# Two decoder layers with routed experts on one core: later row ids, a split first gate/up product, 112-column slot tables

## The reference

```python
scores = jax.nn.sigmoid(xt @ router_w)               # 512 tokens x 16 experts
group  = argmax over 4 groups of the sum of the two best biased scores
expert_idx = the two best experts of that group      # 2 of 16 for each token
w = scores[expert_idx]; w = w / sum(w)
for e in range(16):
    h = silu(xt @ w_gate[e]) * (xt @ w_up[e])        # 1024 -> 512
    y = y + gates[:, e:e + 1] * (h @ w_down[e])      # 512 -> 1024
```

## Time and profile before

| | |
|---|---|
| Median of 3 runs | 1144.84 us (1144.48 to 1145.73) |
| The profiled execution: its own time | 1144.45 us |
| Its span, first to last instruction | 1142.8 us |
| TensorE (PE) busy | 1105.0 us, 97% |
| VectorE (DVE) busy | 836.7 us, 73% |
| ScalarE (ACT) busy | 663.3 us, 58% |
| GpSimd (POOL) busy | 89.7 us, 8% |
| Granted TensorE clock, mean | 0.993 |
| DMA | 295.96 MB, 259 GB/s over the span |

### The profile page before, as it was taken

The page is one execution under the profiler, slowest core; times in us unless marked ns, Lnnn a source line. Parts: engine busy times, 40 slices in busy tenths (PEclk is TensorE's granted clock), DMA queues, the critical chain, the costliest instruction groups (busy, mean ns, idle before and its releaser), DMA issues.

```text
span 1142.8 us, 15358 instructions
## 1 busy us (share of the span) xinstructions
PE 1105.0 (97%) x5434; PEld 872.0 (76%) x5434; DVE 836.7 (73%) x1023; ACT 663.3 (58%) x761; POOL 89.7 (8%) x104
## 2 busy tenths in 40 slices
PE   6999999899999999999999999999989999999995
PEld 5888888567777777777888888888757777777773
DVE  4543556789999999988616555536779999998996
ACT  4322323568888888863417332213548888887872
POOL 2000000111111111010000000000101111111113
PEclk9999999999999999999999999999999999999998
DMA  9925421699999999987304222430499999999985
GB/s 337 384 74 221 147 93 52 217 360 404 382 382 388 378 387 382 391 280 253 134 32 169 89 74 83 169 118 37 154 327 372 388 374 386 381 370 389 378 274 148
DMA packets 51752, 295.96 MB, mean 259 GB/s; under 512 B 8932, under 2 KB 9092, under 8 KB 22128
## 3 DMA queue, kind: packets, MB, share of 16 engines
q1 hardware_dynamic: 35232, 249.58, 57.1%
q0 software_dynamic: 9328, 21.96, 6.9%
q10 hardware_dynamic: 7136, 23.71, 5.5%
HBM read 277.07 MB, written 29.62 MB: 268 GB/s over the span
## 4 chain that ended last, share of the span: by engine, by line
PE 88%; DMA 6%; DVE 3%; ACT 1%; issue 1%; ACTq 0%; DVEq 0%; SPq 0%; POOLq 0%
PE ps L481 26%; PE ps L483 26%; PE ps L482 26%; DMA X<-y_rows 4%; PE ps L1918 2%; PE ps L2133 1%; PE ps L2001 1%; PE ps L1824 1%; DMA y_rows<-y,odx 1%; PE ps L1941 1%; PE ps L1842 1%; DVE lo L477 1%; DMA raw<-in_w_moe 1%; PE ps L1813 1%; DVE hot L518 1%
## 5 line engine op out<-in xcount | busy, mean ns | idle before, releaser
L477 DVE TENSOR_TENSOR lo<-raw,hi 128x1024 fp32r<-128x1024 f32 x320 | 378.6, 1221 | 90.6 <-ACT hi L466 89.1
L466 ACT ACTIVATE hi<-raw 128x1024 fp32r<-128x1024 f32 x320 | 331.2, 1058 | 135.0 <-PE ps L483 99.0
L481 PE MATMUL ps<-hi,xgT_hi 128*112 128x512 f32 x480 | 190.6, 397 | 0.0
L483 PE MATMUL ps<-hi,xgT_lo 128*112 128x512 f32 x480 | 189.1, 394 | 0.0
L482 PE MATMUL ps<-lo,xgT_hi 128*112 128x512 f32 x480 | 187.9, 391 | 0.0
L477 DVE TENSOR_TENSOR lo<-raw_more,hi 128x1024 fp32r<-128x1024 f32 x128 | 154.9, 1222 | 15.9 <-ACT hi L466 7.9
L466 ACT ACTIVATE hi<-raw_more 128x1024 fp32r<-128x1024 f32 x128 | 134.6, 1058 | 33.9 <-PE ps L483 23.3
L481 PE MATMUL ps<-xT_hi,hi 128*128 128x512 f32 x320 | 127.5, 398 | 8.9 <-DVE lo L477 8.9
L482 PE MATMUL ps<-xT_lo,hi 128*128 128x512 f32 x320 | 125.4, 392 | 0.0
L483 PE MATMUL ps<-xT_hi,lo 128*128 128x512 f32 x320 | 125.3, 392 | 0.0
L483 PEld LDWEIGHTS ps<-hi,xgT_lo 128*112 128x112 f32 x480 | 84.0, 175 | 26.4
(11 more groups left out here) (209 smaller groups left out, 1445.2 us busy)
## 6 DMA issues: line engine op xcount, KB each, us to landing
raw<-in_w_moe SPq DMA_DIRECT2D x128, 1024.0 KB, 10.5
raw_more<-in_w_moe SPq DMA_DIRECT2D x64, 1024.0 KB, 10.8
raw<-in_w_dense SPq DMA_DIRECT2D x39, 1024.0 KB, 5.6
y_rows<-X ACTq DMA_DIRECT2D x4, 2048.0 KB, 24.9
X<-y_rows POOLq DMA_DIRECT2D x12, 512.0 KB, 11.6
x_rows<-X ACTq DMA_DIRECT2D x8, 512.0 KB, 2.6
xT_raw<-in_x_t SPq DMA_DIRECT2D x4, 512.0 KB, 6.4
X<-in_x SPq DMA_DIRECT2D x1, 2048.0 KB, 10.0
```

Source lines behind the costliest of these rows:

```text
L466: nc.scalar.activation(hi[:, s, :], flat(raw_units(n)), ACT.Copy).then_inc(hi_ready, 1)
L477: eng.tensor_tensor(lo[:, s, :], flat(raw_units(n)), hi[:, s, :], ALU.subtract).then_inc(lo_ready, 1)
L481: nc.tensor.matmul(out_, a_hi, b_hi, start=first, stop=False)
L483: return nc.tensor.matmul(out_, a_lo, b_hi, start=False, stop=last)
```

## The change

Five things, in both layers:

1. `other_ids` and `route_ids(layer, False)` go. `gates_to_slots` multiplies all 7 columns of `tok_par` instead of 4, and `slot_gates` reads all 7 and makes `idx` of experts 3 to 15 too. POOL's fetch of expert 3 and all after it wait for that.
2. In `gate_up_first`, units 0 to 5 are multiplied as before; then `turn_x(1)` comes, then the gate halves of units 6 and 7, then their up halves. `silu(0)` waits for the gate halves alone (`half_done`), `hidden(0)` for all.
3. `sum_by_slot` takes 112 columns of a table as weights, and `slots_hot` writes 112 of each 128; what follows works on 112 partitions.
4. ACT issues the two DMAs of `ffn_par` after the loop over the experts, just ahead of the last turns, instead of at the start of the experts.
5. Order on ACT and VectorE: `x_hi(1)`, `silu(0)`, the split of unit 4 of expert 1, `h_hi(0)`, then the splits of units 5 to 7. `route_gates` is cut in two: its first four instructions (`gate_values`) come ahead of `hidden(0)`, the other nine (`gate_parts`) where it was.

```diff
         def slots_hot(eng, out_, pos, t, es=slice(0, E)):
-            return eng.tensor_tensor(out_[:, es, :], iota_s[:, None, :].to_broadcast([P, n, P]),
-                                     pos[:, t, es, None].to_broadcast([P, n, P]), ALU.is_equal)
+            return eng.tensor_tensor(out_[:, es, 0:T], iota_s[:, None, 0:T].to_broadcast([P, n, T]),
+                                     pos[:, t, es, None].to_broadcast([P, n, T]), ALU.is_equal)
...
                 def silu(c, step=0, i=0):
-                    act.wait_ge(unit_used, at(INDEX, gu0(layer, c) + GU - 1, step, i) + 1)
+                    if is_zero(c):
+                        act.wait_ge(half_done, 2 * layer + 1)
+                    else:
+                        act.wait_ge(unit_used, at(INDEX, gu0(layer, c) + GU - 1, step, i) + 1)
...
                 preload(ACT.Silu)
-                params(layer, 1, ffn_par[layer])
...
-                for k in range(4, GU):
-                    split_hi(act, gu0(layer, 1) + k)
                 x_hi(1)
                 silu(0)
+                split_hi(act, gu0(layer, 1) + 4)
                 h_hi(0)
+                for k in range(5, GU):
+                    split_hi(act, gu0(layer, 1) + k)
...
+                params(layer, 1, ffn_par[layer])
                 load = heavy(act, layer)
                 last_turns()
...
             def slot_gates(layer):
                 dve.wait_ge(gates_by_slot, layer + 1)
-                chain.step(nc.vector.tensor_copy(scr[layer]["by_slot"][:, :, 3:7],
-                                                 ps[:, 7, 0:4 * E].rearrange("p (e a) -> p e a", a=4)))
+                chain.step(nc.vector.tensor_copy(scr[layer]["by_slot"][0:T, :, :],
+                                                 ps[0:T, 7, 0:7 * E].rearrange("p (e a) -> p e a", a=7)))
+                rows_by_slot(chain, layer, slice(NA, E)).then_inc(idx_ready, 1)
+                dve.wait_ge(idx_ready, 2 * layer + 2)
                 out_rows(chain, layer)
...
-                route_ids(layer, False)
                 route_most(layer)
                 x_lo(1)
+                gate_values(layer)
                 hidden(0)
-                for k in range(4, GU):
+                own_lo(gu0(layer, 1) + 4)
+                h_lo(0)
+                for k in range(5, GU):
                     own_lo(gu0(layer, 1) + k)
-                h_lo(0)
-                route_gates(layer)
+                gate_parts(layer)
...
-                    ins = nc.tensor.matmul(ps[:, bank, n * e:n * (e + 1)], onehot[:, e, :],
+                    ins = nc.tensor.matmul(ps[0:T, bank, n * e:n * (e + 1)], onehot[:, e, 0:T],
...
             def gates_to_slots(layer):
                 pe.wait_ge(gates_done, layer + 1)
                 for t in range(NT):
-                    ins = sum_by_slot(hot[layer][t], 7, t, 3, 4)
+                    pe.wait_ge(hot_ready, 2 * NT * layer + NT + t + 1)
+                    ins = sum_by_slot(hot[layer][t], 7, t, 0, 7)
...
-                    for k in range(GU):
-                        n = gu0(layer, 0) + k
-                        wait_raw(pe, n)
-                        for h in range(2):
-                            ins = nc.tensor.matmul(...)
-                        ins.then_inc(unit_used, 1)
+                    for k in range(GU - 2):
+                        wait_raw(pe, gu0(layer, 0) + k)
+                        product(k, 0)
+                        product(k, 1).then_inc(unit_used, 1)
                         if k == 4:
                             counts(layer)
-                            other_ids(layer)
-                        if k == GU - 2:
-                            turn_x(1)
+                    turn_x(1)
+                    wait_raw(pe, gu0(layer, 0) + GU - 1)
+                    product(GU - 2, 0)
+                    product(GU - 1, 0).then_inc(half_done, 1)
+                    for k in (GU - 2, GU - 1):
+                        product(k, 1).then_inc(unit_used, 1)
```

More of the change, by code:

```diff
@@ L490, in hybrid_decoder @@
         IDA = (7, 3)
-        IDR = (3, 7)
         NA = 3
@@ L526, in rows_by_slot @@
-            return nc.vector.scalar_tensor_tensor(out=idx[:, es], in0=by[:, es, 0], scalar=no_row[:, 0:1],
-                                                  in1=by[:, es, 1], op0=ALU.add, op1=ALU.add)
+            chain.step(nc.vector.scalar_tensor_tensor(out=by[0:T, es, 0], in0=by[0:T, es, 2], scalar=no_row[0:T, 1:2],
+                                                      in1=by[0:T, es, 0], op0=ALU.mult, op1=ALU.add))
+            return nc.vector.scalar_tensor_tensor(out=idx[0:T, es], in0=by[0:T, es, 0], scalar=no_row[0:T, 0:1],
+                                                  in1=by[0:T, es, 1], op0=ALU.add, op1=ALU.add)
@@ L601, in expert @@
                 q = e + E * (turn - 1)
[L602 to L605, removed]
+                src = idx[0:T, e:e + 1] if isinstance(e, int) else idx[0:T, bass.ds(e, 1)]
+                chain.post(nc.gpsimd.tensor_copy(idx_col[0:T, 0:1], src))
+                dst = odx[0:T, e:e + 1] if isinstance(e, int) else odx[0:T, bass.ds(e, 1)]
+                chain.step(nc.gpsimd.tensor_copy(out_col[0:T, 0:1], dst))
                 used = q * EP
@@ L1423, in place_slots, with route_ids @@
                 slots_hot(dve, hot[layer][t], posm, t, slice(0, NA)).then_inc(hot_ready, 1)
[L1425 to L1429, removed]
-                                                 ps[:, bank, 3 * es.start:3 * es.stop].rearrange("p (e a) -> p e a", a=3)))
+            def route_ids(layer):
+                es, bank = slice(0, NA), IDA[layer]
+                dve.wait_ge(ids_ready, layer + 1)
+                chain.step(nc.vector.tensor_copy(scr[layer]["by_slot"][0:T, es, 0:3],
+                                                 ps[0:T, bank, 3 * es.start:3 * es.stop].rearrange("p (e a) -> p e a", a=3)))
                 rows_by_slot(chain, layer, es).then_inc(idx_ready, 1)
@@ L1437, in route_most, with gate_values @@
                 nc.vector.tensor_copy(most[:, layer:layer + 1], scr[layer]["most_f"][:, :]).then_inc(most_ready, 1)
-            def route_gates(layer):
+            def gate_values(layer):
                 gates, gsum = scr[layer]["gates"], scr[layer]["gsum"]
@@ L1493, in hidden @@
                     dve.wait_ge(silu_ready, plus(c + m0 + 1, i))
+                    if is_zero(c):
+                        dve.wait_ge(unit_used, gu0(layer, 0) + GU)
                     if c + m0:
@@ L1853, in first_ids @@
                     ins.then_inc(ids_ready, 1)
-            def other_ids(layer):
-                for t in range(NT):
-                    pe.wait_ge(hot_ready, 2 * NT * layer + NT + t + 1)
-                    ins = sum_by_slot(hot[layer][t], IDR[layer], t, 0, 3, range(NA, E))
-                ins.then_inc(ids_ready, 1)
             def counts(layer):
```

31 lines of the change are left out of this document (16 added, 15 removed).

## The result

| | before | after |
|---|---|---|
| Median of 3 runs | 1144.84 us | 1164.16 us (1163.16 to 1166.40) |
| The profiled execution: own time, span | 1144.45, 1142.8 us | 1163.16, 1161.5 us |
| PE, DVE, ACT, POOL busy | 1105.0, 836.7, 663.3, 89.7 us | 1109.7, 837.6, 665.0, 111.6 us |

A forecast was written before the change was run, and what follows sets the result against it. The prediction took TensorE, 88% of the chain, as the bound, with the DMA also full. Terms of -2.7 us (layer 0) and -3.5 (layer 1) made -6.2, so 1138.6 us on the median's scale; range 1133.3 to 1143.0.

The forecast's parts named there:

- What waits for those ids later: POOL's fetch of expert 3 waits for slot_gates: margin some 3 us, cost nothing, up to 1 us if slow.
- What it saves there is kept to the end, if nothing else holds it: Start of the experts: TensorE never stops once the pipeline runs, so time saved there lasts to the end.
- my sum: Terms of both layers added: -2.7 us in layer 0, -3.5 in layer 1, together -6.2 us.
- The tail: Layer ends: late ffn_par's 1 MB meets the last scatter; 0.7 us taken in each layer, between 0 and 2.
- this rival: Layer ends: last scatter shares the DMA with ffn_par and lands late, 5.0 us lost per layer: 1147.2 us, chance 0.06.
- Weight loads: gates_to_slots: 64 matmuls with 112-column weights take 3.8 us instead of 1.63, 2.2 us more in each layer.
- The rival that they hide: gates_to_slots: dearer weight loads overlap matmuls, so 4.4 us more are gained: 1134.2 us, chance 0.12.
- The clock: Falls behind layer 0's stop and layer 1's turn_h(0) counted as gone, 1.7 us each; least certain of the gains.
- falls elsewhere: Clock falls behind the longer gates_to_slots stretch in both layers, 1.7 us each: 1142.0 us, chance 0.17.
- the stop of `other_ids`: Start of experts: row ids of experts 3 to 15 leave TensorE's path, gaining 3.3 us in each layer.
- the wait before `turn_h(0)`: TensorE's stop falls to 0.8 us: 0.6 less in layer 0, 1.4 in layer 1; gate_values nothing, at worst 0.3.
- The weights don't follow: Later experts: the full DMA's weight ring sets TensorE's arrival, losing the start's gain: about 0, 1144.8 us, chance 0.10.

The follow-up runs named there:

- x3_wait_for_pool: The changed kernel, with VectorE waiting ahead of its four lo and four hot until POOL has issued its gathers of experts 1 and 2: 1149.15 us, ratio 1.0051.
- x4_small_gaps: The changed kernel with a small VectorE memset, waited for, behind each of the four lo of expert 1's units: 1147.17 us, ratio 1.0026.
- y1_idx_112: x5_all_but_112 with only the instruction that makes idx, and its reader for odx, on 112 partitions: 1162.28 us, ratio 1.0154 to the kernel before.
- x5_all_but_112: The changed kernel without the whole of part 3 (tables, row ids and gates on 128 again): 1143.17 us, ratio 0.9985 to the kernel before.
- b6_slots_112: The kernel before with part 3 alone (112-column tables, and what follows on 112 partitions): 1148.69 us, ratio 1.0029.
- x6_par_early_128: The kernel before with parts 1, 2 and 5 alone, so 128 slots and ffn_par early: 1137.20 us, ratio 0.9935.
- b4_par_late: The kernel before with only the two DMAs of ffn_par moved behind the loop over the experts: 1153.30 us, ratio 1.0081.
- x1_par_early: The changed kernel with the two DMAs of ffn_par back at the start of the experts: 1157.76 us, ratio 1.0132 to the kernel before.
- b8_split_only: The kernel before with parts 2 and 5 alone: 1143.84 us, ratio 0.9990.

## Why the prediction was wrong, step by step

**The failed step: "What waits for those ids later" and the costing of part 3.** I costed part 3 as weight loads only, and of POOL I looked at the wait of expert 3's fetch and at landings of 11 us, never at what POOL's issuing instruction takes and what lets it run. No rival of mine was this. One line of part 3, the row ids on 112 partitions, makes the gather 9.7 us longer to issue. Its price is its exposure, that is, how much of it TensorE has to wait for: without the hold the changed kernel is 15.0 us faster in x3_wait_for_pool and 17.0 in x4_small_gaps; in y1_idx_112 against x5_all_but_112 it costs 19.1 us; in b6_slots_112, behind `other_ids`, nearly nothing. In the changed kernel it is 6.80 + 0.82 + 0.81 = 8.4 us in layer 0 (wait, transposes, products against 0.93 and x5's 3.60) and 6.27 + 0.83 + 2.36 = 9.5 in layer 1.

The Trainium skill ("SBUF — State Buffer", section "Who interferes with whom") states that a VectorE instruction with two inputs in SBUF contends with a GpSimd instruction that reads SBUF. The trace agrees on who holds whom: all eight instructions under the gather have two SBUF inputs, POOL takes 11.51 us under them and 1.0 to 1.2 where VectorE waits. The same section says that `tensor_tensor` was not seen to stall a DMA; here a chain of `tensor_tensor` holds up the instruction that issues one. It also has the lock held for one instruction; here POOL was passed over at seven boundaries. In both the measurement decides. That the shared port is what POOL waits for is the page's reason; the runs show only that VectorE's chain holds it.

**"What it saves there is kept to the end, if nothing else holds it."** Something else did, in layer 0: the scatter and the two accumulating DMAs behind it. I read them as the place of `ffn_par` only. In x6, with `ffn_par` early, layer 0's 5.3 us are gone by layer 1, so that of the loops' gain only layer 1's 6.2 is left: the span is 5.7 shorter. (The profiled execution is the slowest of its six; the median is 7.8 shorter, against 1144.96 for the kernel before on the same chip, so some executions keep more.) That is also why x6_par_early_128 came out 4 us above the 1133 of its expectation. So my sum fails without the hold too. For the parts in x5_all_but_112 it says -12.0 + 1.4 = -10.6; x5 measured -1.7. Its loops gain what I forecast, 5.5 and 6.2 us, and its tails take 6.1 and 4.5 back.

**The tail (term +0.7 a layer): right side, size off.** Three pairs of kernels differ in the place of `ffn_par` alone. Early and late, in us:

| | scatter of layer 0 | from it to layer 1's first gather | from the last scatter of layer 1 to the end | median |
|---|---|---|---|---|
| before, b4_par_late | 6.06, 9.39 | 336.7, 343.0 | 45.2, 47.9 | +8.5 |
| x1_par_early, the changed kernel | 5.01, 9.22 | 335.9, 343.3 | 43.9, 45.6 | +6.4 |
| x6_par_early_128, x5_all_but_112 | 8.56, 9.38 | 342.5, 342.8 | 45.1, 49.7 | +6.0 |

I had 1.4 us for both layers; it is 6.0 to 8.5 by the medians (4 to 9 by the ratios). I had priced the scatter alone, and by how empty the DMA was in its last 2 us; the two accumulating DMAs behind it take part (36.5 us for the three in b4_par_late, 32.3 before). With `ffn_par` late the scatter of layer 0 lands after 9.2 to 9.4 us, just short of the 9.8 at which I let this rival decide. But the place of `ffn_par` is not all of it: with it early, the stretch behind layer 0's scatter is 336.7 us in the kernel before and 342.5 in x6. What else sets it stays open.

**Weight loads (+2.2): right, a little smaller.** After, beside the earlier trace rows:

```profile
L1877 PEld LDWEIGHTS ps<-tok_par,hot 128*112 128x112 bf16 x76 | 4.5, 132 | 0.2
```

```profile
248.31 3.43 PE L1877 MATMUL ps<-tok_par,hot 128*112 128x7 bf16 x64
251.60 0.63 PE L1988 MATMUL ps<-ident_b,hot 128*112 128x128 bf16 x8
```

3.29 us, 51 ns each, 1.66 us more than before. In y1_idx_112, 7 columns with weights of 128 take 1.63 us, so the width of the weights alone does it. The rival that they hide is out.

**The clock.** The old falls went where no other stop came (x5, x6: 1.00 in both windows). The rival "falls elsewhere" came true in layer 1 of the changed kernel, behind `gates_to_slots`:

```profile
874.90:884.00 9.10, 9.10 (x47) 7.42 (x47) 8.65 (x15) 6.76 (x7) 4.14 (x2) 0.81 0.98 379
```

9.10 x 0.19 is 1.7 us, its price. In layer 0 that place stays at full clock; in x4_small_gaps, part 3 without the hold, the clock falls there in both layers (0.66 over 240.00 to 250.00, 0.74 over 850.00 to 862.00), in x5 and x6, with 128 columns, in neither. But b8_split_only has 128 columns and a fall there too, so the 112 columns are not the only way to it.

**Right:** the stop of `other_ids` is gone; the wait before `turn_h(0)` is 0.88 and 0.95 us (0.8 forecast), `gate_values` included; fetch 3 is issued at 254.93 and nobody waits for it. **The weights don't follow:** not seen, no wait for weights in the loops.

**The account of layer 1**, from the first product (834.58) to the last scatter (1115.92), 6.2 us more than before: -6.2 (as x6) + 9.5 (hold) + 1.7 (loads) + 1.7 (clock) = +6.7. In layer 0, from 212.52 to 491.63, it is 4.7 more: -5.5 + 8.4 + 1.7 = +4.6.

## What to carry to other kernels

Before giving an earlier stop away, look at what it covers: read each engine's instruction that feeds the next wait, and ask what it would take if its neighbour did not let it in. A duration that differs between rows of the same form (1.77 against 0.99 us) is the sign of such a neighbour. Where GpSimd issues DMAs that TensorE soon needs, read its rows after every edit near them, even one of a single line; here a one-column memset within or ahead of VectorE's row of two-input instructions, or VectorE's wait until GpSimd had issued, was enough. And a gain ahead of a chain of dependent DMAs can be lost in it.

## What the runs showed of the hardware that was not expected

- GpSimd's indirect DMA instruction for expert 1 (such an instruction takes 1.0 to 1.2 us where VectorE waits) took 11.4 to 12.4 us in seven kernels and both layers, each time until about 1 us behind the last of eight back-to-back VectorE instructions with two SBUF operands; in eleven others it got in at the first boundary (1.66 to 1.79 us).
- Which of the two happened followed a `scalar_tensor_tensor` on 112 instead of 128 partitions, some 0.7 us earlier on VectorE, and was undone by a one-column memset of 0.06 us behind it.
- 64 matmuls that move 7 columns, each with bf16 weights of its own, follow each other at 51 ns with 112 weight columns and at 25.5 ns with 128.
